# Hybrid retention and RG-LRU decoder step: state growths placed inside the last gate projection, last state products ahead of the second state half, low halves of the recurrent stage on VectorE

## The chip, the cores and the metric

The kernel runs on one core of a Trainium2 chip. The metric is the device time of one launch in microseconds (us). TensorE runs the matrix products, VectorE and ScalarE the elementwise work, GpSimd a few elementwise pieces and the transfers of the states, and SyncE the transfers of the weights. In the rows, PE is TensorE, PEld its weight loads, DVE VectorE, ACT ScalarE, POOL GpSimd and SP SyncE.

## The reference, cut to what matters

One inference step of a two-layer trunk over 528 prompt tokens (16 meta tokens and 512) and 8 running sequences of 8 tokens. Each layer does the following.

```python
xn = rmsnorm(x, ln_g)
q, k, v, z_a, x_b, z_b, g_a, g_b = split(xn @ w_in)
# retention, 4 heads, dk 256, dv 512
scores = (q @ k.T) * decay
o = scores @ v + (q * gq) @ S          # S: the state of each sequence
S_new = gamma**L * S + (k * kdecay).T @ v
o_a = group_norm(o, gn_g) * silu(z_a)
# RG-LRU, width 1536, gates block-diagonal in blocks of 96
xc = conv4(x_b);  r, i = sigmoid(xc @ w_r + b_r), sigmoid(xc @ w_i + b_i)
a = exp(-8 * r * softplus(-lam));  h = scan(a, sqrt(1 - a*a) * i * xc)
x = x + (sig(g_a) * ((o_a) @ w_a) + sig(g_b) * ((h * silu(z_b)) @ w_b)) @ w_o
```

## The kernel before, in words

All 592 tokens (528 prompt, 64 sample) are held transposed, features on the partitions, in two halves of 296 columns. Every product is made in three matmuls: each fp32 operand x is split into a rounded `x_hi` and a remainder `x_lo = x - x_hi`, and the product is hi·hi + lo·hi + hi·lo (helpers `three`, L1234 to L1239, and `three_of`, L1290 to L1294). ScalarE makes the high halves by a copy, VectorE (in places GpSimd) the low halves by a subtraction.

The order of the work is written out by hand, one instruction list for each engine, joined by semaphores. Weights come as units of 128x1024 in a ring of four (`w_raw`, `w_hi`, `w_lo`): SyncE loads one as soon as the unit four places before is used, ScalarE rounds it (`split_hi`, L354), VectorE subtracts (`split_lo`, L362), and TensorE waits for that. Results go to a ring of four PSUM banks in a fixed list of jobs (`phases`, L146): job n uses bank n mod 4 and waits until job n - 4 has been read out.

**Head stage** (four heads in each of two layers, some 150 us each). TensorE runs 16 units for each head: projections 0 to 10 (q, k, v, and three quarters of the gate z), 11 (the last quarter of z), then the output product w_a. The recurrent states of the eight sequences pass through four slots of the tile `S`, in pairs. Growing a pair has two halves c = 0 and c = 1 (`grow`, L1324 on TensorE, L808 on VectorE): TensorE makes k.T v of both sequences in two PSUM banks, VectorE computes S * gamma^8 + that in place, and TensorE may make the next product only when VectorE has read the one before (`grown_free`). After half c = 1 GpSimd stores the pair and loads the next two states into the same slots (L439 to L447). The product of the queries with the states (`cross`, L1311) accumulates in its own bank `o_last`, two sequences at a time: pairs 0 and 1 early, pairs 2 and 3 late. In the old order TensorE does, after projection 10: `grow(1, 0)` (L1376), `inner` 0 and 1 (the scores times v of the prompt blocks), `grow(1, 1)` (L1381), `inner` 2 and 3, the scores times v for `o_last`, `prompt_state(0)`, `cross(2)`, `prompt_state(1)`, `cross(3)` (L1408 to L1411), then four transposed blocks `oT` of the normalized output (L1413 to L1419), projection 11 in two halves with `oT` 4 between, and w_a. VectorE, beside it: the silu of z (L819), `grow` 1,0 (L954), the variance of output blocks 0 and 1, `grow` 1,1 (L984), the variance of blocks 2 and 3 (`variance`, L956), normalization of blocks 0 to 3, the variance of block 4 (the rows of `o_last`), then `gate` (L977), which multiplies `oT` with silu(z) and frees the bank. ScalarE copies both halves of the prompt state, and then `o_last` (L615 to L621).

**Recurrent stage** (two passes `it` of two groups `g` in each layer). TensorE makes three projections for the convolution and three for the gate z_b (six units), and then the block-diagonal gate products (L1453 to L1467), which wait for the low halves of the gate weights (`gwl_ready`) and of the convolved tiles (`xcl_ready`). ScalarE copies the projections out, rounds `xc_hi` and `gw_hi`, and evaluates tanh, sigmoid, exp and sqrt. VectorE makes the convolution (`conv`, L1081: a TENSOR_SCALAR at L1094, then three SCALAR_TENSOR_TENSOR) and the silu (L1108, which frees the bank of z_b) in the order conv 0, conv 1, silu 0, conv 2, silu 1, silu 2, then the products with the gates and the scans (L1125 to L1157). GpSimd makes `gw_lo` (L482, 128x1792) and three `xc_lo` (L487, 128x592 each) for each group, and loads the gate weights (`load_gates`, L470).

Then come the gates g_a and g_b, the w_b product and the output product w_o, which the change does not touch.

Of the kernel before, what the change touches and what calls it, by code (L numbers as in the profile page):

```python
# [27 lines left out]
D_MODEL, DEPTH, SEQ, N_META = 1024, 2, 512, 16  # L28
DEC_BATCH, DEC_SEQ, PAST_LEN = 8, 8, 4096
HEADS, DK, DV = 4, 256, 512  # L30
# [10 lines left out]
LT = LRU // P  # L41
GROUPS = 4
# [141 lines left out]
def trunk(nc, x_in, w_units, gate_w, packs, final_gain, consts, decay, state_ret,  # L184
          y_out, ret_p, ret_s, conv_out, h_out):
    f32, f32r = mybir.dt.float32, mybir.dt.float32r
# [5 lines left out]
    with ctx:  # L192
# [144 lines left out]
        def apart(eng):  # L337

            eng.sem_inc(passed, 1)
# [60 lines left out]
        def _(pool):  # L400
# [14 lines left out]

            for l in range(DEPTH):
                pool.wait_ge(xn_ready, l * KT + KT)
                pool.wait_ge(x_stored, l * 16 + 16)
                apart(pool)
                pool.memset(qz[:, :, :], 0.0).then_inc(qz_clear, 1)  # L420
                for h in range(HEADS):
                    hh = l * HEADS + h
# [55 lines left out]
                load_gates(1)  # L478
                for g in range(GROUPS):
                    pool.wait_ge(gwh_ready, l * GROUPS + (g + 1))  # L480
                    apart(pool)
                    pool.tensor_tensor(gw_lo[:, g % 2, :, :], gw[:, g % 2, :, :],  # L482
                                       gw_hi[:, :, :].bitcast(f32), SUB).then_inc(gwl_ready, 1)
                    for t in range(3):
                        pool.wait_ge(xch_ready, l * LT + g * 3 + (t + 1))
                        apart(pool)
                        pool.tensor_tensor(xc_lo[:, t, :], xc[:, t, :], xc_hi[:, t, :].bitcast(f32), SUB)\  # L487
                            .then_inc(xcl_ready, 1)
                    if g + 2 < GROUPS:
                        load_gates(g + 2)  # L490
                pool.wait_ge(ob_ready, l * LT + LT)
# [24 lines left out]
        def _(act):  # L516
# [17 lines left out]

            for l in range(DEPTH):
                root(l + 1)
# [4 lines left out]

                for h in range(HEADS):
                    hh = l * HEADS + h
# [71 lines left out]
                    for c in range(2):  # L615
# [3 lines left out]
                        act.drain().then_inc(sp_ready, 1)  # L619
                    act.wait_ge(o_last_full, hh + 1)  # L620
                    act.activation(o_tok[:, 4, :], o_last[:, :], ACT.Copy).then_inc(oraw_ready, 1)  # L621
                    for k, piece in enumerate(PIECES):
# [13 lines left out]
                act.activation(tiny[:, 1, :], tiny[:, 0, :], ACT.Exp, scale=-1.0).then_inc(lamexp_ready, 1)  # L636
                for it in range(2):
                    for g in range(2):
# [65 lines left out]
                for ph in ("GA", "GB"):  # L704
                    if ph == "GB":
                        act.wait_ge(ob_ready, l * LT + LT)
                        for k in range(LT):
                            act.activation(ob_hi[:, k, :], ob[:, k, :], ACT.Copy).then_inc(obh_ready, 1)
                    for it in range(2):
                        for i in range(4):  # L710
                            for n, (a, b) in enumerate(HALVES):
                                name = (("proj", i), n)
                                if ph == "GB":
                                    act.wait_ge(ga_used, l * 16 + it * 8 + (i * 2 + n + 1))
                                wait_job(act, ph, l, it, name)
                                apart(act)
                                act.activation(sg[:, ds(it * 4 + i, 1), a:b].rearrange("p o t -> p (o t)"),
                                               psum_of(ph, name)[:, 0:HALF], ACT.Tanh, scale=0.5)\
                                   .then_inc(freed(ph, name), 1)
                                act.drain().then_inc(ga_ready if ph == "GA" else gb_ready, 1)  # L720
                            split_hi(act, ph, l, it, i)
                done = 0
                for m in range(KT):
# [5 lines left out]
                    if m % 2 == 0 or m == KT - 1:  # L729
                        split_hi(act, "B", l, 0, done)  # L730
                        done += 1
                for it in range(2):
                    for i in range(4):
                        n = l * KT + it * 4
                        act.wait_ge(sqs_ready, n + (KT + i - 1))
                        act.wait_ge(x_ready, n + (KT + i + 1))
                        apart(act)
                        act.activation(sq[:, i % 2, :], xT[:, ds(it * 4 + i, 1), :].rearrange("p o t -> p (o t)"),
                                       ACT.Square).then_inc(sq_ready, 1)
                        split_hi(act, "O", l, it, i)  # L740
# [4 lines left out]
        def _(dve):  # L745
# [30 lines left out]

            for l in range(DEPTH):
                dve.drain()
# [25 lines left out]

                for h in range(HEADS):
                    hh = l * HEADS + h
# [24 lines left out]
                    for i in range(11):  # L831
                        if i < 4:
# [31 lines left out]
                            if i == 3:  # L864
                                dve.wait_ge(ret_stored, hh + 1)
                                dve.memset(ks_src[:, :, 24:32].bitcast(f32), 0.0)
                                dve.memset(vs_src[:, :, :, 24:32].bitcast(f32), 0.0)
                                for c in range(2):
                                    dve.tensor_tensor(
                                        ks_tmp[:, c * 8:c * 8 + 8, :],  # L870
                                        qk[:, 2 + c, TP:T].rearrange("p (b x) -> p b x", b=8),
                                        cst[:, ds(h * DEC_SEQ + C_GK, DEC_SEQ)].rearrange("p (o x) -> p o x", o=1)
                                        .to_broadcast([P, 8, 8]), MUL)
                                dve.drain().then_inc(kg_ready, 1)
                        elif i >= 8:
                            silu(i)
# [76 lines left out]
                        if i == 10:  # L953
                            grow(1, 0)  # L954

# [25 lines left out]

                    for j in range(2):
                        variance(j, False)
                    grow(1, 1)  # L984
                    variance(2, False)
                    variance(3, True)
# [90 lines left out]

                for it in range(2):
                    for g in range(2):
# [28 lines left out]
                        def silu(t):  # L1108
# [8 lines left out]
                            split_lo(dve, "L", l, it, g * 6 + 3 + t)  # L1117

                        conv(0)
                        conv(1)  # L1120
                        silu(0)
                        conv(2)
                        silu(1)
                        silu(2)
                        for t in range(3):  # L1125
# [32 lines left out]

                for it in range(2):
                    for i in range(4):  # L1160
# [7 lines left out]
                for k in range(LT):  # L1168
                    dve.wait_ge(obh_ready, l * LT + (k + 1))
                    dve.tensor_tensor(ob_lo[:, k, :], ob[:, k, :], ob_hi[:, k, :].bitcast(f32), SUB)\  # L1170
                       .then_inc(obl_ready, 1)
                for it in range(2):
                    for i in range(4):
                        split_lo(dve, "GB", l, it, i)
# [28 lines left out]
                apart(dve)  # L1203
                for it in range(2):
                    part = sqs[:, ds(it, 1), :].rearrange("p o t -> p (o t)")
# [27 lines left out]
        def _(pe):  # L1233
# [62 lines left out]
            pe.wait_ge(const_in, 32)  # L1296
            for l in range(DEPTH):
                square_sums(l)
                for h in range(HEADS):
                    hh = l * HEADS + h  # L1300
# [34 lines left out]
                    project_first("R", l, h, xn_ready)  # L1335
                    for i in range(2, 11):
                        project("R", l, h, ("proj", i), i)
# [24 lines left out]
                        if i == 9:  # L1362
# [3 lines left out]
                            for n, (j, a, b) in enumerate(SCORE_JOBS):  # L1366
# [7 lines left out]
                                done("R", name, ins)  # L1374
                            grow(0, 1)
                    grow(1, 0)  # L1376
                    pe.wait_ge(vtok_ready, hh + 1)
                    pe.wait_ge(sc_ready, hh + 1)
                    for i in range(4):
                        if i == 2:  # L1380
                            grow(1, 1)  # L1381
                        name = ("inner", i)
# [25 lines left out]
                    prompt_state(0)  # L1408
                    cross(2)
                    prompt_state(1)  # L1410
                    cross(3)  # L1411
                    pe.wait_ge(on_ready, hh * 2 + 1)
# [34 lines left out]

                for it in range(2):
                    for g in range(2):
# [18 lines left out]
                for ph in ("GA", "GB"):  # L1468
                    for it in range(2):
                        for i in range(4):  # L1470
                            project(ph, l, it, ("proj", i), i)
                waited = 0
                for m in range(KT):
# [3 lines left out]
                    for n, (a, b) in enumerate(HALVES):  # L1477
# [8 lines left out]
                        done("B", name, ins)  # L1486
                for it in range(2):
                    project_first("O", l, it, mgl_ready)
                    for i in range(2, 4):
                        project("O", l, it, ("proj", i), i)  # L1490
# [106 lines left out]
```

## Time and profile before

| What | before |
|---|---|
| median of three runs | 2171.89 us (2171.14 to 2172.06) |
| the profiled execution | 2171.74 us |
| its span | 2169.9 us, 34433 instructions |
| TensorE busy | 2079.1 us (96%), mean granted clock 0.988 |
| VectorE, ScalarE, GpSimd busy | 1203.2, 757.4, 250.1 us |

How to read it: the span runs from the first to the last instruction of the profiled execution, which took 1.8 us more than its span. A row of a timeline gives the start, the duration, the engine, the line, the operation and its tiles, and in brackets how long the engine sat idle before it and for whom. Matmuls overlap, so a matmul's duration is longer than the distance to the next one's start.

### The profile page before, as it was taken

How to read it: one execution, taken by the hardware profiler on the slowest of the kernel's cores; microseconds unless marked ns; L12 is line 12 of the kernel's file. 1: busy time of each engine (PE TensorE's matmuls, PEld its weight loads, DVE VectorE, ACT ScalarE, POOL GpSimd, SP SyncE). 2: the span in 40 equal slices, each digit the busy share in tenths (PEclk: the TensorE clock that was granted, in tenths of full speed). 3: DMA queues.
4: the chain of work that ended last, by engine and by line, in shares of the span. 5: the costliest groups of instructions: out<-in, count | busy, mean ns of one | idle time of the engine just before them, and what ended most of it. 6: DMA issues, size and time to landing. Idle time of an engine off the chain costs nothing.

```text
span 2169.9 us, 34433 instructions
## 1 busy us (share of the span) xinstructions
PE 2079.1 (96%) x14368; PEld 1945.7 (90%) x14368; DVE 1203.2 (55%) x2035; ACT 757.4 (35%) x1260; POOL 250.1 (12%) x247
## 2 busy tenths in 40 slices
PE   4999999999999999999989999999999999999997
PEld 4979979889799999999988898997997998999996
DVE  5455455454557777524474555545646677763345
ACT  3421322322325655422233223233232355654222
POOL 1021020020112211000000201202102211100000
PEclk8999999999999999999999999999999999999998
DMA  5234243233342211322232333333423421232223
GB/s 214 69 122 156 71 135 139 101 113 122 117 156 76 76 59 59 132 69 88 88 142 95 115 131 122 109 111 108 170 64 126 151 76 66 69 113 78 69 98 139
DMA packets 60267, 234.04 MB, mean 108 GB/s; under 512 B 6944, under 2 KB 6944, under 8 KB 59472
## 3 DMA queue, kind: packets, MB, share of 16 engines
q1 hardware_dynamic: 37584, 137.41, 18.9%
q0 software_dynamic: 22528, 94.43, 12.0%
q8 instruction: 113, 1.85, 0.3%
q14 instruction: 42, 0.34, 0.1%
HBM read 183.92 MB, written 47.89 MB: 107 GB/s over the span
## 4 chain that ended last, share of the span: by engine, by line
PE 83%; DVE 6%; ACT 4%; DVEq 3%; issue 2%; ACTq 1%; DMA 1%; SPq 0%
PE bank L1237 23%; PE bank L1239 22%; PE bank L1238 22%; PE bank L1292 4%; PE bank L1294 3%; PE bank L1293 3%; PE o_last L1319 3%; DVEq L1145 2%; DVE rr L1149 2%; PE sums L1331 1%; PE bank L1308 1%; ACT rr L698 1%; DMA w_raw<-in_w_units 1%; ACTq L697 1%; DVE ct L1098 1%
## 5 line engine op out<-in xcount | busy, mean ns | idle before, releaser
L1237 PE MATMUL bank<-xn_hi,w_hi 128*128 128x296 f32 x3072 | 927.3, 302 | 47.8 <-DVE xn_lo L788 22.1
L1239 PE MATMUL bank<-xn_lo,w_hi 128*128 128x296 f32 x3072 | 922.9, 300 | 0.0
L1238 PE MATMUL bank<-xn_hi,w_lo 128*128 128x296 f32 x3072 | 919.9, 299 | 0.0
L1237 PEld LDWEIGHTS bank<-xn_hi,w_hi 128*128 128x128 f32 x3072 | 582.5, 190 | 71.3 <-issue 57.4
L1238 PEld LDWEIGHTS bank<-xn_hi,w_lo 128*128 128x128 f32 x3072 | 583.3, 190 | 0.0
L1239 PEld LDWEIGHTS bank<-xn_lo,w_hi 128*128 128x128 f32 x3072 | 580.9, 189 | 0.0
L366 DVE TENSOR_TENSOR w_lo<-w_raw,w_hi 128x1024 fp32r<-128x1024 f32 x248 | 311.4, 1256 | 336.6 <-ACT w_hi L360 332.9
L360 ACT ACTIVATE w_hi<-w_raw 128x1024 fp32r<-128x1024 f32 x248 | 261.6, 1055 | 323.5 <-DMA w_raw<-in_w_units 317.5
L1237 PE MATMUL bank<-oa_hi,w_hi 128*128 128x296 f32 x512 | 156.7, 306 | 0.0
L1239 PE MATMUL bank<-oa_lo,w_hi 128*128 128x296 f32 x512 | 153.6, 300 | 0.0
L1238 PE MATMUL bank<-oa_hi,w_lo 128*128 128x296 f32 x512 | 152.4, 298 | 0.0
L435 POOL DMA_DIRECT2D out_ret_s<-S x64 | 45.7, 717 | 849.2 <-DVEq L817 848.8
L1239 PE MATMUL bank<-ob_lo,w_hi 128*128 128x296 f32 x384 | 115.2, 300 | 0.0
L1237 PE MATMUL bank<-ob_hi,w_hi 128*128 128x296 f32 x384 | 114.6, 298 | 0.0
L1238 PE MATMUL bank<-ob_hi,w_lo 128*128 128x296 f32 x384 | 114.2, 297 | 0.0
L1237 PEld LDWEIGHTS bank<-oa_hi,w_hi 128*128 128x128 f32 x512 | 96.3, 188 | 7.8 <-issue 7.7
L1037 DVE TENSOR_TENSOR acc<-bank,acc 128x296 f32<-128x296 f32 x128 | 58.9, 465 | 71.0 <-PE bank L1239 70.2
L1238 PEld LDWEIGHTS bank<-oa_hi,w_lo 128*128 128x128 f32 x512 | 96.7, 189 | 0.0
L1239 PEld LDWEIGHTS bank<-oa_lo,w_hi 128*128 128x128 f32 x512 | 96.5, 188 | 0.0
L814 DVE SCALAR_TENSOR_TENSOR S<-S,cst,sums 128x512 f32<-128x512 f32 x128 | 89.8, 743 | 1.7 <-PE sums L1331 1.7
L565 ACT ACTIVATE vo<-bank 128x296 f32<-128x296 f32 x64 | 26.7, 417 | 152.8 <-PE bank L1239 152.0
L826 DVE SCALAR_TENSOR_TENSOR zz<-zz,bank 128x296 f32<-128x296 f32 x64 | 29.6, 462 | 79.2 <-ACT zz L550 78.3
(204 smaller groups left out, 2753.0 us busy)
## 6 DMA issues: line engine op xcount, KB each, us to landing
w_raw<-in_w_units SPq DMA_DIRECT2D x251, 512.0 KB, 3.3
S<-in_state_ret POOLq DMA_DIRECT2D x64, 512.0 KB, 4.7
out_ret_s<-S POOLq DMA_DIRECT2D x64, 512.0 KB, 4.0
gw<-in_gate_w POOLq DMA_DIRECT2D x8, 896.0 KB, 5.3
x_scr<-xT POOLq DMA_DIRECT2D x3, 2368.0 KB, 8.3
xT<-x_scr POOLq DMA_DIRECT2D x2, 2368.0 KB, 11.3
out_ret_p<-Sp POOLq DMA_DIRECT2D x8, 512.0 KB, 3.9
dec<-in_decay POOLq DMA_DIRECT2D x9, 264.0 KB, 3.2
```

The source lines that it names most:

```text
L360: act.activation(w_hi[:, n % RING, :], w_raw[:, n % RING, :], ACT.Copy).then_inc(unit_hi, 1)
L366: dve.tensor_tensor(w_lo[:, n % RING, :], w_raw[:, n % RING, :], w_hi[:, n % RING, :].bitcast(f32), SUB).then_inc(unit_lo, 1)
L435: pool.dma_start(dst, S[:, s, :, :]).then_inc(s_out[s], 16)
L814: dve.scalar_tensor_tensor(S[:, s, c, :], S[:, s, c, :], cst[:, ds(h + C_G8, 1)], grown[i][:, :], MUL, ADD).then_inc(grown_free, 1)
L1037: dve.tensor_tensor(acc[:, m, a:b], psum_of("R", name)[:, 0:HALF], acc[:, m, a:b], ADD)\
L1237: pe.matmul(ps, w_hi[:, slot, cols], x_hi, start=first, stop=False)
L1238: pe.matmul(ps, w_lo[:, slot, cols], x_hi, start=False, stop=False)
L1239: return pe.matmul(ps, w_hi[:, slot, cols], x_lo, start=False, stop=last)
L1292: pe.matmul(ps, left_hi, right_hi, start=first, stop=False)
L1293: pe.matmul(ps, left_lo, right_hi, start=False, stop=False)
L1294: return pe.matmul(ps, left_hi, right_lo, start=False, stop=last)
L1319: ins = pe.matmul(o_last[at:at + QUAD, :], qz[:, c, b * QUAD:b * QUAD + QUAD], S[:, s, c, :], start=(n < 4 and c == 0), stop=(n >= 4 and c ...
```

## The change

In the head stage, projection 10 is made half by half on TensorE, with `grow(1, 0)` between the halves and `grow(1, 1)` after the second; VectorE takes its parts of the two growths right after the silu of the first half and after the weight subtraction that follows the second. `cross(3)` comes directly after `cross(2)`, ahead of `prompt_state(1)`, and ScalarE copies `o_last` between the two halves of the prompt state. In the recurrent stage the four subtractions of a group (`gw_lo` and three `xc_lo`) leave GpSimd's list and stand in VectorE's, between the convolutions and the silus; GpSimd keeps only the loads of the gate weights. In a number of loops `range(n)` is written `range(0, n)`, which counts the same; these lines are left out here.

```diff
@@ GpSimd
                 load_gates(0)
                 load_gates(1)
-                for g in range(GROUPS):
-                    pool.wait_ge(gwh_ready, l * GROUPS + (g + 1))
-                    apart(pool)
-                    pool.tensor_tensor(gw_lo[:, g % 2, :, :], gw[:, g % 2, :, :],
-                                       gw_hi[:, :, :].bitcast(f32), SUB).then_inc(gwl_ready, 1)
-                    for t in range(3):
-                        pool.wait_ge(xch_ready, l * LT + g * 3 + (t + 1))
-                        apart(pool)
-                        pool.tensor_tensor(xc_lo[:, t, :], xc[:, t, :], xc_hi[:, t, :].bitcast(f32), SUB)\
-                            .then_inc(xcl_ready, 1)
-                    if g + 2 < GROUPS:
-                        load_gates(g + 2)
+                load_gates(2)
+                load_gates(3)
@@ ScalarE
                         act.drain().then_inc(sp_ready, 1)
-                    act.wait_ge(o_last_full, hh + 1)
-                    act.activation(o_tok[:, 4, :], o_last[:, :], ACT.Copy).then_inc(oraw_ready, 1)
+                        if c == 0:
+                            act.wait_ge(o_last_full, hh + 1)
+                            act.activation(o_tok[:, 4, :], o_last[:, :], ACT.Copy).then_inc(oraw_ready, 1)
@@ VectorE
+                        elif i == 10:
+                            silu(i, (0,))
+                            grow(1, 0)
+                            silu(i, (1,))
                         elif i >= 8:
                             silu(i)
...
                         if i == 10:
-                            grow(1, 0)
+                            grow(1, 1)
...
-                    for j in range(2):
+                    for j in range(3):
                         variance(j, False)
-                    grow(1, 1)
-                    variance(2, False)
                     variance(3, True)
...
+                        def low_xc(t):
+                            dve.wait_ge(xch_ready, gg * 3 + (t + 1))
+                            dve.tensor_tensor(xc_lo[:, t, :], xc[:, t, :], xc_hi[:, t, :].bitcast(f32), SUB)\
+                               .then_inc(xcl_ready, 1)
+
                         conv(0)
                         conv(1)
                         silu(0)
+                        low_xc(0)
                         conv(2)
+                        low_xc(1)
                         silu(1)
+                        dve.wait_ge(gwh_ready, gg + 1)
+                        dve.tensor_tensor(gw_lo[:, g, :, :], gw[:, g, :, :], gw_hi[:, :, :].bitcast(f32), SUB)\
+                           .then_inc(gwl_ready, 1)
+                        low_xc(2)
                         silu(2)
@@ TensorE
-                    for i in range(2, 11):
+                    for i in range(2, 10):
                         project("R", l, h, ("proj", i), i)
...
+                    project("R", l, h, ("proj", 10), 10, (0,))
                     grow(1, 0)
+                    project("R", l, h, ("proj", 10), 10, (1,))
+                    grow(1, 1)
...
                     for i in range(4):
-                        if i == 2:
-                            grow(1, 1)
                         name = ("inner", i)
...
                     prompt_state(0)
                     cross(2)
+                    cross(3)
                     prompt_state(1)
-                    cross(3)
```

## Rows read from the trace of the kernel before

**Rows 1.** The profile's page: busy time of each engine, share of the span, instructions.

```profile
PE 2079.1 (96%) x14368; PEld 1945.7 (90%) x14368; DVE 1203.2 (55%) x2035; ACT 757.4 (35%) x1260; POOL 250.1 (12%) x247
```

**Rows 2.** TensorE's waits: line, waited for; us in total, times, longest us.

```profile
PE bank L1237 <- DVE w_lo L366: 12.3, 4, 5.0
PE sums L1331 <- DVE S L814: 10.5, 8, 1.3
PE bank L1237 <- DVE zl L1114: 7.1, 4, 1.8
PE bank L1237 <- DVE oa L979: 6.1, 8, 0.8
```

**Rows 3.** TensorE's timeline, first head: both old growths, then `prompt_state(1)`.

```profile
122.65 0.50 PE L1331 MATMUL sums<-vst,kst 24*128 24x512 f32 x2
...
125.03 0.40 PE L1294 MATMUL bank<-vtok_lo,sc_hi 128*128 128x512 f32 x1
126.75 0.50 PE L1331 MATMUL sums<-vst,kst 24*128 24x512 f32 x2 [1.32 <-DVE S L814]
...
141.16 0.50 PE L1292 MATMUL bank<-vtok_hi,ktok_hi 128*128 128x512 f32 x1
```

**Rows 4.** VectorE's timeline, first head.

```profile
121.06 0.46 DVE L826 SCALAR_TENSOR_TENSOR zz<-zz,bank 128x296 f32<-128x296 f32 x1
...
125.29 1.40 DVE L814 SCALAR_TENSOR_TENSOR S<-S,cst,sums 128x512 f32<-128x512 f32 x2
...
128.83 1.41 DVE L814 SCALAR_TENSOR_TENSOR S<-S,cst,sums 128x512 f32<-128x512 f32 x2
...
147.60 0.69 DVE L959 BATCH_NORM_STATS2 stats<-vo 128x6 f32<-128x512 f32 x1 [7.18 <-ACT vo L621]
```

**Rows 5.** GpSimd's timeline, first head: the second pair of states.

```profile
130.90 1.43 POOL L435 DMA_DIRECT2D out_ret_s<-S  x2 [6.65 <-DVEq L817]
...
136.58 0.72 POOL L430 DMA_DIRECT2D S<-in_state_ret  x1 [0.46 <-issue]
```

**Rows 6.** Landing times of transfers: L430 in 134 to 139 us; all of `S`.

```profile
DMA to landing us min/median/max: 3.7/4.3/4.9
...
DMA to landing us min/median/max: 3.2/4.3/10.5
```

**Rows 7.** TensorE's timeline, recurrent stage of the first layer.

```profile
720.27 0.37 PE L1237 MATMUL bank<-xn_hi,w_hi 128*128 128x296 f32 x1 [1.76 <-DVE zl L1114]
...
763.44 0.61 PE L1237 MATMUL bank<-xn_hi,w_hi 128*128 128x296 f32 x1 [4.99 <-DVE w_lo L366]
```

**Rows 8.** Windows: length; busy (instructions) of PE, PEld, DVE, ACT, POOL; granted clock, DMA.

```profile
763.40:785.50 22.10, 22.06 (x145) 22.06 (x146) 18.28 (x24) 7.33 (x11) 5.87 (x3) 0.88 0.16 49
870.99:890.30 19.31, 19.31 (x142) 19.31 (x143) 8.44 (x14) 4.79 (x8) 1.57 (x3) 1.00 0.60 232
```

**Rows 9.** GpSimd's timeline, second group of the first layer.

```profile
701.69 4.16 POOL L482 TENSOR_TENSOR gw_lo<-gw,gw_hi 128x1792 fp32r<-128x1792 f32 x1 [13.88 <-ACT gw_hi L667]
...
720.75 2.21 POOL L487 TENSOR_TENSOR xc_lo<-xc,xc_hi 128x592 fp32r<-128x592 f32 x1 [4.24 <-ACT xc_hi L673]
```

**Rows 10.** VectorE's timeline, the same stretch.

```profile
701.86 4.62 DVE L1140 TENSOR_TENSOR ii<-ii,rr 128x592 f32<-128x592 f32 x1
...
710.51 0.60 DVE L1094 TENSOR_SCALAR ct<-xpad,lp 128x616 f32<-128x616 f32 x1
...
713.95 1.22 DVE L366 TENSOR_TENSOR w_lo<-w_raw,w_hi 128x1024 fp32r<-128x1024 f32 x1
...
719.66 0.83 DVE L1114 SCALAR_TENSOR_TENSOR zl<-zl,bank 128x296 f32<-128x296 f32 x2
...
721.73 1.57 DVE L1094 TENSOR_SCALAR ct<-xpad,lp 128x616 f32<-128x616 f32 x1
```

**Rows 11.** VectorE's lines by form: busy, mean ns | idle before.

```profile
L947 DVE TENSOR_TENSOR sc_lo<-sc,sc_hi 128x1600 fp32r<-128x1600 f32 x8 | 14.6, 1825 | 2.1 <-ACTq L608 2.1
L1170 DVE TENSOR_TENSOR ob_lo<-ob,ob_hi 128x592 fp32r<-128x592 f32 x24 | 16.6, 772 | 0.2
```

More of the change, by code:

```diff
@@ L414, in power @@
                                    ALU.pow).then_inc(rsd_ready, 1)
-            for l in range(DEPTH):
+            for l in range(0, DEPTH):
                 pool.wait_ge(xn_ready, l * KT + KT)
@@ L420, in _ @@
                 pool.memset(qz[:, :, :], 0.0).then_inc(qz_clear, 1)
-                for h in range(HEADS):
+                for h in range(0, HEADS):
                     hh = l * HEADS + h
@@ L533, in _ @@
                 act.activation(w_hi[:, i, :], w_raw[:, i, :], ACT.Copy).then_inc(unit_hi, 1)
-            for l in range(DEPTH):
+            for l in range(0, DEPTH):
                 root(l + 1)
@@ L540, in _ @@
                 act.wait_ge(x_stored, l * 16 + 16)
-                for h in range(HEADS):
+                for h in range(0, HEADS):
                     hh = l * HEADS + h
@@ L636, in _ @@
                 act.activation(tiny[:, 1, :], tiny[:, 0, :], ACT.Exp, scale=-1.0).then_inc(lamexp_ready, 1)
-                for it in range(2):
+                for it in range(0, 2):
                     for g in range(2):
@@ L708, in _ @@
                             act.activation(ob_hi[:, k, :], ob[:, k, :], ACT.Copy).then_inc(obh_ready, 1)
-                    for it in range(2):
+                    for it in range(0, 2):
                         for i in range(4):
@@ L731, in _ @@
                         done += 1
-                for it in range(2):
+                for it in range(0, 2):
                     for i in range(4):
@@ L775, in _ @@
                 dve.tensor_tensor(w_lo[:, i, :], w_raw[:, i, :], w_hi[:, i, :].bitcast(f32), SUB).then_inc(unit_lo, 1)
-            for l in range(DEPTH):
+            for l in range(0, DEPTH):
                 dve.drain()
@@ L802, in _ @@
                 apart(dve)
-                for h in range(HEADS):
+                for h in range(0, HEADS):
                     hh = l * HEADS + h
@@ L1076, in _ @@
                 dve.tensor_scalar(lam_nc[:, :], u[5], -LRU_C, None, MUL).then_inc(par_ready, 1)
-                for it in range(2):
+                for it in range(0, 2):
                     for g in range(2):
@@ L1157, in _ @@
                                .then_inc(ob_ready, 1)
-                for it in range(2):
+                for it in range(0, 2):
                     for i in range(4):
@@ L1171, in _ @@
                        .then_inc(obl_ready, 1)
-                for it in range(2):
+                for it in range(0, 2):
                     for i in range(4):
@@ L1203, in _ @@
                 apart(dve)
-                for it in range(2):
+                for it in range(0, 2):
                     part = sqs[:, ds(it, 1), :].rearrange("p o t -> p (o t)")
@@ L1296, in _ @@
             pe.wait_ge(const_in, 32)
-            for l in range(DEPTH):
+            for l in range(0, DEPTH):
                 square_sums(l)
-                for h in range(HEADS):
+                for h in range(0, HEADS):
                     hh = l * HEADS + h
@@ L1446, in _ @@
                 apart(pe)
-                for it in range(2):
+                for it in range(0, 2):
                     for g in range(2):
@@ L1468, in _ @@
                 for ph in ("GA", "GB"):
-                    for it in range(2):
+                    for it in range(0, 2):
                         for i in range(4):
@@ L1486, in _ @@
                         done("B", name, ins)
-                for it in range(2):
+                for it in range(0, 2):
                     project_first("O", l, it, mgl_ready)
```

## The prediction

> **What bounds the kernel now.** I read the page first: TensorE is busy 96% of the span and VectorE 55% [rows 1], so a change that leaves the matmuls as they are can only win what TensorE waits. The next view is therefore who TensorE waits for [rows 2]. Four kinds of wait lie in the stages that the change touches, 36.0 us in all: for the growth on VectorE (8 times, once in each head), for `gate` (8), for the silu of the recurrent stage (4) and for low halves of weights (4, of which two are 5.0 us long). Then the timelines around each wait. In a head, TensorE stands before the second growth until VectorE has read the first [rows 3], and VectorE reads it late because that stands behind both silus and a weight subtraction of projection 10 [rows 4]. Further on, VectorE sits idle 7.18 us for ScalarE's copy of `o_last` [rows 4], which comes after `cross(3)`; the variance of block 4 then stands in front of `gate`, and projection 11 waits for the bank that `gate` frees, 6.1 / 8 = 0.76 us [rows 2]. In the recurrent stage TensorE waits 1.76 us for a silu and 4.99 us for a weight [rows 7]. VectorE is the late one there, and two of its rows say why: a 128x592 product took 4.62 us [rows 10] where another subtraction of that size takes 0.77 [rows 11]. It was issued 0.17 us after GpSimd began its `gw_lo` of 4.16 us [rows 9] and ended 0.6 us after that one's end. L1094 took 0.60 us once, and 1.57 where it met an `xc_lo` that ran from 720.75 to 722.96 us; it ended 0.3 us after that [rows 9, 10]. So GpSimd's subtractions hold VectorE up, by 4.62 - 0.77 = 3.85 us and by 0.97 us.
>
> **How a wait becomes lost time.** The idle time is counted from the modelled end of the matmul before. A 296-column matmul starts 19.31 / 142 = 0.136 us after the one before [rows 8] and lasts about 0.30, so a wait there costs its idle time and 0.16 more: 1.92 us for the silu and 5.15 us for the weight [rows 7]. The other two weight waits are (12.3 - 10.0) / 2 = 1.15 us idle [rows 2], 1.31 us lost. Among 512-column matmuls the step is 0.136 x 512 / 296 = 0.235 us, and across the wait for the growth 126.75 - 125.03 = 1.72 us pass [rows 3]: 1.49 us lost.
>
> **Part 1, the growths inside projection 10.** Nothing is added; the same four matmuls and four VectorE operations of a head move. TensorE's first growth came after projection 10 at 122.65 us and took 0.43 us to the next start (0.50 [rows 3] less the overlap); now it lies between the halves, so TensorE stands before the second growth at 122.65 + 0.43 = 123.1 us. VectorE was free for the silu of the first half at 121.06 us [rows 4]; the growth follows it some 0.4 us later and takes 1.40 us [rows 4]: read at 122.9. The 1.49 us goes, by a margin of 0.2 us, so tenths may come back. Behind the growths on VectorE stands the variance, and that has cover: VectorE idles there later anyway [rows 4].
>
> **Part 2, the last state products first.** `cross(3)` comes the 15 matmuls of `prompt_state(1)` earlier, 15 x 0.235 = 3.5 us. ScalarE then copies `o_last` under them, VectorE takes the variance of block 4 in the 7.18 us that it idled [rows 4], and `gate` follows the first transposed block at once. The 0.76 us before projection 11 goes. Two things could be late next. ScalarE now waits for `o_last` ahead of its copy of the second state half, which frees the bank of `oT` 3; what covers it is `prompt_state(1)` for the wait, and for the copy only the twelve transposes of `oT` 0 to 2, which no row here prices (third rival). And `cross(3)` needs states 6 and 7. VectorE's second growth takes the place of the first, 125.29 + 0.43 us, and ends at 127.1 where it ended at 130.24 [rows 4]. GpSimd's store of the pair began at 130.90 us and its second load at 136.58 [rows 5], 5.7 us later; that load landed in at most 4.9 us more [rows 6]. All 3.1 us earlier, the states are there at 138.4 us at the latest. TensorE reaches `cross(3)` where `prompt_state(1)` began, 141.16 - 1.49 = 139.7 us [rows 3]: 1.3 us of slack, and no cost in the sum. GpSimd's `pow` for the normalization, queued behind those transfers, is 3.1 us earlier with them.
>
> Parts 1 and 2 together give 1.49 + 0.76 = 2.25 us for a head, 18.0 us for eight.
>
> **Part 3, four subtractions on VectorE.** Removed: every hold-up by GpSimd in this stage. Added to VectorE for each group: three `xc_lo` at 0.77 us [rows 11] (0.69 from start to start) and one `gw_lo` of 1792 columns. The trace has no VectorE subtraction that wide; 592 columns take 0.772 and 1600 take 1.825 us [rows 11], 1.045 ns a column, so 1.825 + 192 x 0.001045 = 2.03 us. Below it the bound is 1.83, above it the 4.16 us that GpSimd needs [rows 9]; I take 2.03, as the row of 1600 is the nearest. The wait for `gw_hi` that VectorE's list gains costs nothing: GpSimd had it at 701.69 us [rows 9], VectorE comes to it after 723. GpSimd's loads of gate weights wait for the same signal as before.
>
> What this does to TensorE, group 2 of a layer: the silu that it waited for began at 719.66 us [rows 10]. Without 3.85 and 0.97 us of hold-up (a convolution before it met an `xc_lo` too) it begins at 714.84, before TensorE wants the bank at 720.27 - 1.92 = 718.35: the wait of 1.92 us goes, twice in a layer (groups 2 and 4). Then VectorE runs silu and weight 2.07 us (721.73 - 719.66), `xc_lo` 0.69, the convolution 3.44 (713.95 - 710.51), `xc_lo` 0.69, silu and weight 2.07 [rows 10], `gw_lo` 2.03, together 10.99 us. That ends at 725.8 us; TensorE would begin the gate products at 718.35 + 48 x 0.136 = 724.9 us, so a new wait of some 0.9 us stands before them. I take 0.8, since 2.07 includes a pause ahead of a convolution that the second silu does not have. Group 1 has the slack of a stage just begun, as the four silu waits [rows 2] are those of groups 2 and 4; groups 2 to 4 pay 2.4 us. At the border of the passes the weight subtraction stands behind the scans; they start 3.85 us earlier, so of 5.15 us 1.30 remain, just what the last group shows at the next border, where GpSimd has nothing to subtract (1.31). After the long wait the granted clock was 0.88 over 22.10 us, so part of it ran at 1.2 GHz: 145 matmuls took 22.10 in place of 145 x 0.136 = 19.72 us. After the short wait it was 1.00 [rows 8]. These 2.38 us go too. A layer gains 2 x 1.92 + 3.85 + 2.38 - 2.4 = 7.7 us, both 15.3 us.
>
> **The sum.** 18.0 + 15.3 = 33.3 us off the profiled execution's 2171.74 us gives 2138.4 us. That execution is 0.15 us under the median of the runs. A measurement of this kernel can tell about 0.2%, 4.3 us, from no change.
>
> **The rivals.**
> VectorE keeps up (0.17): `gw_lo` and the `xc_lo` cause no waits at all and the border wait closes too. Then 2 x (2.4 + 1.30) = 7.4 us more go: 2131 us. For it: VectorE's stage is some tenths from meeting TensorE. Against: the 1.31 us at a border without GpSimd's work.
>
> VectorE becomes the bound of the recurrent stage (0.12): its new operations cost 4.16 us instead of 2.03, and L1094 stays at 1.57 because its slowness is its own. Then 2.1 + 1.0 us come on top in six groups, 18.7 us: 2157 us. Against: the same line took 0.60 us when GpSimd was still, and with the hold-ups gone VectorE's list for a group is shorter, not longer (3.85 + 2 x 0.97 off, 2.03 + 3 x 0.69 on). A rule of the Trainium skill speaks for it (Perfetto Trace Analysis, section Optimizing Scalar/DVE Operations): where VectorE is saturated, handing work to GpSimd may pay; by it the four subtractions stood in the right place and the time would be this rival's. The trace agrees that VectorE is the late engine here, not that GpSimd relieves it.
>
> Only half of the head's gain comes (0.07): the growth is read some tenths late or the bank of `oT` 3 is, 1 us in each head, 2146 us.
>
> The states land late (0.04), the other side: `cross(3)` starts 5.0 us sooner (3.5 and the 1.49 of part 1), the loads only 3.1 us. It decides once a load lands more than 6.2 us after its issue (4.9 of the row and 1.3 of slack). The slowest state transfer of the run took 10.5 us [rows 6]: then TensorE waits 4.3 us in each head, 34.4 us, and if the clock falls after it as it does after 4.99 us, 8 x 2.38 = 19 us more: 2138.4 + 53.4 = 2192 us, slower than before. Against: in that stretch the loads landed in 3.7 to 4.9 us [rows 6].
>
> **How the numbers follow.** The forecast as summed gets 0.60: 2138.4 us. The range takes in it, the first and the third rival, and tenths of a microsecond of error in each wait: 2129 to 2150 us. It leaves out 0.16. All cases but the last are faster by over 0.2%: 0.95, no change 0.01, slower 0.04.
>
> **What would show it.** Right: no wait of TensorE for L814 and `gate` left; the head's repeat 2.2 us shorter; L1140 at 0.78 and L1094 at 0.60 us throughout; waits of TensorE for the gates' low halves of about 0.8 us in three groups of four; 1.3 us at each border with the clock at 1.00 after it. Wrong: a wait of the products with `S` for the transfer, a `gw_lo` on VectorE well over 2.1 us, or gate waits of several microseconds.

## The result and the profile after

The changed kernel takes 2122.1 us (median of four runs, 2121.34 to 2122.95) against 2171.73 us of the kernel before, a median of four too: ratio 0.9772, with a 95% interval of 0.9755 to 0.9789. That is 49.6 us less where 33.3 were forecast, and below the range's lower end of 2129. The profiled execution took 2121.34 us, its span is 2119.6. In the profile of the changed kernel TensorE's lines stand 4 (from L1417 on 5) higher and VectorE's between 9 lower and 4 higher than before.

The page and TensorE's waits (line, waited for; us in total, times, longest us), to be laid beside [rows 1, 2]:

```profile
PE 2056.9 (97%) x14368; PEld 1939.2 (91%) x14368; DVE 1188.8 (56%) x2067; ACT 758.2 (36%) x1260; POOL 169.8 (8%) x215
...
PE bank L1241 <- DVE w_lo L366: 4.6, 4, 1.1
PE bank L1296 <- DVE gw_lo L1125: 3.6, 6, 1.0
```

Same number of matmuls, and yet TensorE's busy time fell by 22.2 us, more than the 2 x 2.38 us that the prediction gave to the clock: waits alone cannot explain the gain. The waits for the growth, for `gate` and for the silu are gone, as forecast, and so are the 5.0 us waits for a weight. The new wait for `gw_lo` is there too.

Where the busy time went is seen in TensorE's lines by form, first of the kernel before, then of the changed one (busy us, mean ns | idle before):

```profile
L1319 PE MATMUL o_last<-S,qz 128*32 128x512 f32 x256 | 61.1, 598 | 0.0
```

```profile
L1323 PE MATMUL o_last<-S,qz 128*32 128x512 f32 x256 | 47.6, 598 | 0.0
```

The 256 rows of the products with the states (two rows for each of 128 matmuls; the expectations call the rows matmuls) are as long as before, 598 ns, and fill 13.5 us less of the engine's time. TensorE's timeline of the first head shows where, first before, then after:

```profile
139.32 1.91 PE L1319 MATMUL o_last<-S,qz 128*32 128x512 f32 x8
...
145.01 1.91 PE L1319 MATMUL o_last<-S,qz 128*32 128x512 f32 x8
```

```profile
118.60 0.50 PE L1335 MATMUL sums<-vst,kst 24*128 24x512 f32 x2
...
122.50 0.50 PE L1335 MATMUL sums<-vst,kst 24*128 24x512 f32 x2
137.17 1.94 PE L1323 MATMUL o_last<-S,qz 128*32 128x512 f32 x16
142.92 1.97 PE L1422 MATMUL bank<-cst,vo 128*128 128x128 f32 x16
144.64 0.38 PE L1241 MATMUL bank<-xn_hi,w_hi 128*128 128x296 f32 x1
```

The growths wait for nobody (compare 126.75 in [rows 3]), and projection 11 begins at 144.64 without a wait. From one head to the next it is 145.72 us (67.26 to 212.98), where the kernel before has 149.86 (68.05 to 217.91): 4.14 us less, and 2.25 were forecast. The eye should stop at `x16`: both crosses together take 1.94 us, where before each took 1.91 by itself. The second one is almost free. Their rows begin in steps of about 0.43 us. In the first step the kernel before has two rows that start together, and the changed one four:

```profile
139.32 0.62 PE L1319 MATMUL o_last<-S,qz 128*32 128x512 f32 x2
```

```profile
137.17 0.65 PE L1323 MATMUL o_last<-S,qz 128*32 128x512 f32 x4
```

In the recurrent stage of the first layer the waits that are left, and the windows after the border of the passes (columns as in [rows 8]):

```profile
708.31 0.40 PE L1296 MATMUL bank<-xc_hi,gw_hi 128*128 128x296 f32 x1 [0.64 <-DVE gw_lo L1125]
...
740.72 0.41 PE L1241 MATMUL bank<-xn_hi,w_hi 128*128 128x296 f32 x1 [1.14 <-DVE w_lo L366]
...
760.92 0.41 PE L1296 MATMUL bank<-xc_hi,gw_hi 128*128 128x296 f32 x1 [0.36 <-DVE gw_lo L1125]
...
812.38 0.40 PE L1296 MATMUL bank<-xc_hi,gw_hi 128*128 128x296 f32 x1 [0.64 <-DVE gw_lo L1125]
```

```profile
740.72:760.30 19.58, 19.58 (x144) 19.58 (x144) 18.58 (x26) 7.92 (x12) 0.00 (x0) 1.00 0.22 80
```

The long wait of [rows 7] has become 1.14 us, and the granted clock behind it is 1.00, that is 2.4 GHz throughout, where it was 0.88 [rows 8]. VectorE's lines by form say the same from its side:

```profile
L1144 DVE TENSOR_TENSOR ii<-ii,rr 128x592 f32<-128x592 f32 x24 | 18.5, 770 | 0.4
L1125 DVE TENSOR_TENSOR gw_lo<-gw,gw_hi 128x1792 fp32r<-128x1792 f32 x8 | 16.2, 2019 | 0.0
L1087 DVE TENSOR_SCALAR ct<-xpad,lp 128x616 f32<-128x616 f32 x24 | 14.4, 601 | 2.7 <-issue 0.4
```

`gw_lo` takes 2.02 us (2.03 were estimated), and the two lines that GpSimd held up are at 0.77 and 0.60 us throughout.

### The profile page after: what moved, and what is told of

Read it like the earlier page. It is cut to its first block, busy times and chain, and to the rows that moved or that the text cites. A ratio compares the mean times of both kernels' runs of the same rounds, so it can differ in the third digit from the quotient of the medians.

```text
span 2119.6 us, 34409 instructions
## 1 busy us (share of the span) xinstructions
PE 2056.9 (97%) x14368; PEld 1939.2 (91%) x14368; DVE 1188.8 (56%) x2067; ACT 758.2 (36%) x1260; POOL 169.8 (8%) x215
## 4 chain that ended last, share of the span: by engine, by line
PE 82%; DVE 9%; ACT 3%; DVEq 2%; issue 1%; ACTq 1%; DMA 1%; SPq 0%
PE bank L1241 22%; PE bank L1243 21%; PE bank L1242 21%; PE bank L1296 4%; PE bank L1298 4%; PE bank L1297 4%; PE o_last L1323 2%; DVE rr L1153 2%; DVE ct L1091 1%; DVE w_lo L366 1%; PE sums L1335 1%; PE bank L1312 1%; ACT rr L689 1%; DMA w_raw<-in_w_units 1%; ACTq L688 1%
## 5 line engine op out<-in xcount | busy, mean ns | idle before, releaser
L366 DVE TENSOR_TENSOR w_lo<-w_raw,w_hi 128x1024 fp32r<-128x1024 f32 x248 | 303.1, 1223 | 336.7 <-ACT w_hi L360 332.7
L1242 PEld LDWEIGHTS bank<-ob_hi,w_lo 128*128 128x128 f32 x384 | 72.4, 189 | 0.0
```

The source lines that it names most:

```text
L366: dve.tensor_tensor(w_lo[:, n % RING, :], w_raw[:, n % RING, :], w_hi[:, n % RING, :].bitcast(f32), SUB).then_inc(unit_lo, 1)
L1242: pe.matmul(ps, w_lo[:, slot, cols], x_hi, start=False, stop=False)
```

## The experiments

Two theories stood for the surplus. **T1**: the pair of `cross(2)` writes two quarters (32 rows each) of `o_last` and the pair of `cross(3)` the other two, so that next to each other their matmuls run side by side on TensorE. **T2**: `cross(3)` costs what it cost, and the surplus comes from its place, from another part or from how the parts meet.

**Each part alone, and parts 1 and 2 together.** Each kernel is the one before with the hunks of the diff that belong to the part.

> The kernel before with part 1 alone: both growths of the second pair inside and behind projection 10, nothing else moved. By the prediction's term it gains the 1.49 us of the wait for the growth in each of eight heads, 11.9 us: 2171.7 - 11.9 = 2159.8 us, and TensorE's wait for S (10.5 us in eight) is gone. If the surplus of the changed kernel (a head shortened by 4.15 us where 2.25 were forecast) came from this part, it gains 11.9 + 14.4 = 26.3 us: 2145 us.

Measured: 2160.33 us against 2171.39, ratio 0.9953 (0.9936 to 0.9969): 11.1 us less, and the wait for `S` is not in the list any more. Part 1 is what the prediction said; the surplus isn't here.

> The kernel before with part 2 alone: cross(3) directly behind cross(2), ScalarE's copy of o_last between the halves of the prompt state. Theory T1: the two crosses write different quarters of o_last, so their matmuls run beside each other and the second costs almost nothing; the gain of a head is then 0.76 us (the wait for gate) and about 1.8 us (a cross): 8 x 2.56 = 20.5 us, 2151 us, and the sixteen matmuls of both crosses together take about 1.9 us. Rival T2 (cross(3) costs the same wherever it stands, as the prediction had it): 8 x 0.76 = 6.1 us, 2166 us, and the sixteen take 3.7 us.

Measured: 2162.78 us, ratio 0.9962 (0.9948 to 0.9977): 8.6 us less, by the interval 5 to 11. That is not the 20.5 of T1, and the 6.1 of T2 is not excluded. The rows of the products fill 59.1 us, 2.0 less than before; with the 6.1 us for `gate`, whose wait is gone, that makes 8.1. The timeline of this kernel's first head says why, and so do the waits of TensorE's weight loads (us in total, times, longest us):

```profile
139.05 1.91 PE L1320 MATMUL o_last<-S,qz 128*32 128x512 f32 x10
141.50 1.90 PE L1320 MATMUL o_last<-S,qz 128*32 128x512 f32 x6 [0.55 <-DMA S<-in_state_ret]
```

```profile
PEld o_last L1320 <- DMA S<-in_state_ret: 5.9, 7, 1.5
```

Only two of the second cross's rows got beside the first's; then it stood for its other state. GpSimd's timeline of the same head shows the loads of that pair, first in this kernel, then in the changed one:

```profile
135.28 0.71 POOL L430 DMA_DIRECT2D S<-in_state_ret  x1 [3.21 <-DMA out_ret_s<-S]
136.49 0.72 POOL L430 DMA_DIRECT2D S<-in_state_ret  x1 [0.50 <-issue]
```

```profile
131.02 0.71 POOL L430 DMA_DIRECT2D S<-in_state_ret  x1 [2.38 <-DMA out_ret_s<-S]
132.86 0.72 POOL L430 DMA_DIRECT2D S<-in_state_ret  x1 [1.14 <-DMA out_ret_s<-S]
```

The wait ended at 141.50, 5.0 us after the later issue. This is the fourth rival of the prediction, at work where part 1 does not bring the loads forward. The next kernel brings them forward.

> The kernel before with parts 1 and 2 together, part 3 undone. Measured alone, part 1 gave 11.1 us, part 2 8.6 and part 3 17.6, together 37.3 of the 49.3 us of the whole. T1 (side by side crosses, which part 2 alone could not use since its cross(3) waited for state 7, 0.55 us idle in the first head): the two parts together give 49.3 - 17.6 = 31.7 us, 2139.7 us, with sixteen matmuls in about 1.9 us and no wait for a state. Rival T2 (the parts of the head add up, and the surplus lies between head and recurrent stage): 19.7 us, 2151.7 us.

Measured: 2141.35 us against 2171.98, ratio 0.9859 (0.9844 to 0.9873): 30.6 us less, by T1 31.7 and by T2 19.7. The products with the states fill 48.7 us of TensorE's time. Part 2 needs part 1. The expectation of no wait for a state failed: three are left, 0.8 us together.

> The kernel before with part 3 alone: gw_lo and the xc_lo on VectorE. By the prediction's term 2 x 7.7 = 15.3 us less, 2156.4 us; by the difference of the recurrent stages in the two traces (215.20 to 206.37 us in a layer) 17.7 us less, 2154 us. The granted clock stays at 1.00 behind the border of the passes. If part of that difference came from the other parts, it gains less than 15.3 us.

Measured: 2153.82 us against 2171.39, ratio 0.9920 (0.9905 to 0.9934): 17.6 us less. With the 30.6 us of the head that makes 48.2 of the 49.6, so the two stages add up.

**The same order, other quarters.** Begin and end of the sums in `o_last` move with it (the flags of its earlier products, left out here).

```diff
-                                at = b // 2 * QUAD
+                                at = (b // 2 - (2 if pair == 3 else 0)) * QUAD
```

> The changed kernel with cross(3) accumulated into the quarters of o_last that cross(2) writes, and the sums in o_last begun and ended elsewhere to suit, so that the rows of the samples are not the reference's. Order, number and sizes of all instructions stay. T1 (neighbours run beside each other because they write different quarters): the sixteen matmuls take 3.7 us instead of 1.94, 1.75 us more in each head, of which VectorE's part behind them may hide nothing: 8 x 1.75 = 14 us above the changed kernel's 2122.1, 2136 us. Rival T2 (being next to each other is enough, whatever the quarters): 2122 us.

Measured: 2133.73 us, 11.6 us above the changed kernel. The first head:

```profile
137.20 3.63 PE L1323 MATMUL o_last<-S,qz 128*32 128x512 f32 x16
144.60 1.97 PE L1422 MATMUL bank<-cst,vo 128*128 128x128 f32 x16
```

Same place, same sixteen rows, 3.63 us instead of 1.94, and what follows is 1.68 us later. The rows start two at a time again:

```profile
137.20 0.62 PE L1323 MATMUL o_last<-S,qz 128*32 128x512 f32 x2
```

T2 falls: being neighbours is not enough, it takes different quarters. Whether the array of TensorE or the bank sets this, no run here separates. Eight times 1.68 would be 13.4 us. Over all heads the rows fill 59.6 us here and 47.6 in the changed kernel, 12.0 us, near the 11.6 measured. The difference is that this kernel takes 3.63 us in every head, while the changed kernel doesn't reach 1.94 in all of them. In its last head a state lands late:

```profile
1614.18 2.95 PE L1323 MATMUL o_last<-S,qz 128*32 128x512 f32 x16
```

```profile
1610.62 0.71 POOL L430 DMA_DIRECT2D S<-in_state_ret  x1 [0.48 <-issue]
```

The loads of that head took 4.0 to 4.6 us to land, so the later one landed after the rows had begun. Four of the eight heads are above 1.94 (2.10, 1.99, 2.29 and 2.95), 1.6 us in all.

**The same neighbours, old place.**

```diff
                     prompt_state(0)
-                    cross(2)
                     prompt_state(1)
+                    cross(2)
                     cross(3)
```

> The kernel before with both halves of the prompt state first and cross(2), cross(3) behind them: the pair is adjacent but not earlier than before, and nothing else is moved. T1: cross(3) costs almost nothing beside cross(2), 8 x 1.75 = 14 us less than the kernel before, 2157 us; the wait for gate (0.76 us a head) stays. Rival T2 (the gain needs the early place, under which ScalarE and VectorE do the work of block 4): no change, 2171 us.

Measured: 2157.77 us against 2171.98, ratio 0.9935 (0.9920 to 0.9950): 14.2 us less by exchanging two calls, with the waits for `S` and `gate` left nearly as they were (10.5 and 6.4 us). The sixteen rows take 1.94 us in all eight heads. The early place is not needed either.

**The early crosses joined.**

```diff
-                        if i in (5, 6):
-                            if i == 5:
-                                pe.wait_ge(qk_ready, hh * 2 + 1)
-                            cross(i - 5)
+                        if i == 6:
+                            pe.wait_ge(qk_ready, hh * 2 + 1)
+                            cross(0)
+                            cross(1)
```

> The changed kernel with the early crosses joined too: cross(0) leaves its place behind projection 5 and comes directly ahead of cross(1) behind projection 6. T1: cross(1) costs almost nothing, 8 x 1.8 = 14.4 us less than the changed kernel's 2122.1, 2107.7 us. Rival T2: no change, 2122 us; or slower if the first growth, which reads the same states, is put off by the later cross(0).

Measured: 2106.17 us, ratio to the kernel before 0.9699 (0.9683 to 0.9716), 15.9 us under the changed kernel. TensorE's lines by form:

```profile
L1323 PE MATMUL o_last<-S,qz 128*32 128x512 f32 x256 | 33.1, 598 | 0.0
```

61.1, 47.6, 33.1 us with none, one and both couples joined: each is worth about 14 us. T1 foretold this gain too.

**The halves of part 3.** First `gw_lo` alone moves to VectorE, then the three `xc_lo` alone.

```diff
                         silu(1)
+                        dve.wait_ge(gwh_ready, gg + 1)
+                        dve.tensor_tensor(gw_lo[:, g, :, :], gw[:, g, :, :], gw_hi[:, :, :].bitcast(f32), SUB)\
+                           .then_inc(gwl_ready, 1)
                         silu(2)
```

> The kernel before with gw_lo alone on VectorE, behind the second silu; the three xc_lo stay on GpSimd. By the prediction's terms gw_lo is the costly one: its hold-up of 3.85 us goes and with it both silu waits (2 x 1.92 a layer), 3.85 of the border wait and 2.38 of clock; without the xc_lo in VectorE's list the gates wait little. A layer gains about 9 us, 2171.9 - 18 = 2154 us, about as much as the whole of part 3 (17.6). Rival: the xc_lo carry half of it or more, and this kernel gains 9 us or less, 2163 us or above.

Measured: 2171.01 us against 2172.34, ratio 0.9993 (0.9983 to 1.0002). The expectation of 18 us failed. TensorE's waits and then its timeline in this kernel:

```profile
PE bank L1291 <- DVE gw_lo L1121: 14.7, 7, 2.7
```

```profile
726.83 0.41 PE L1291 MATMUL bank<-xc_hi,gw_hi 128*128 128x296 f32 x1 [2.45 <-DVE gw_lo L1121]
```

VectorE's and GpSimd's timelines just before it:

```profile
723.51 3.27 DVE L1121 TENSOR_TENSOR gw_lo<-gw,gw_hi 128x1792 fp32r<-128x1792 f32 x1
```

```profile
722.71 2.19 POOL L483 TENSOR_TENSOR xc_lo<-xc,xc_hi 128x592 fp32r<-128x592 f32 x1 [4.27 <-ACT xc_hi L669]
```

And windows of the same kernel, behind that wait and behind the shorter one at the border:

```profile
726.83:748.88 22.05, 22.05 (x151) 22.05 (x152) 8.72 (x12) 14.97 (x22) 0.57 (x1) 0.92 0.18 66
...
760.73:780.26 19.53, 19.53 (x144) 19.53 (x144) 18.52 (x24) 7.80 (x12) 5.29 (x3) 1.00 0.23 81
```

The silu waits went and the border wait shrank to 1.14 us, as the terms said. But two convolutions of a group still meet an `xc_lo` (1.57 us in place of 0.60), and `gw_lo` now meets the third one itself: 3.27 us in place of 2.02. So the gates wait 2.20 to 2.74 us in three groups of a layer, and the granted clock falls behind each (0.92 over 22.05 us: part of it at 1.2 GHz; 151 matmuls take 22.05 us instead of 151 x 0.136 = 20.5).

> The kernel before with the three xc_lo on VectorE and gw_lo left on GpSimd. By the prediction's terms the hold-up of 3.85 us stays, and with it the 5.0 us wait at the border of the passes and the lower clock behind it; against 0.97 us of hold-up for each xc_lo the list gains 0.69. At best the silu waits shrink, up to 2 x 1.9 us a layer: 0 to 7.6 us less, 2164 to 2172 us. Rival: the xc_lo carry the gain, 2163 us or below.

Measured: 2171.40 us against 2172.34, ratio 0.9995 (0.9985 to 1.0004), at the lower end of what was expected. `gw_lo` on GpSimd still holds VectorE up: its product of `ii` and `rr` has a mean of 1.73 us, as in the kernel before, and 0.77 with `gw_lo` moved.

```profile
L1143 DVE TENSOR_TENSOR ii<-ii,rr 128x592 f32<-128x592 f32 x24 | 41.6, 1735 | 0.4
```

The list of TensorE's waits keeps the long weight waits and spreads the silu's:

```profile
PE bank L1240 <- DVE w_lo L366: 12.6, 4, 5.0
...
PE bank L1240 <- DVE zl L1109: 3.5, 4, 1.1
PE bank L1295 <- DVE zl L1109: 2.6, 4, 0.7
```

Each half gives about 1 us, which its interval does not tell from nothing; both together give 17.6. One half takes GpSimd's work off one place, and the other half meets VectorE in another.

**What is left.** `gw_lo` goes ahead of the weight subtraction inside `silu(1)`:

```diff
-                        silu(1)
+                        silu(1, False)
                         dve.wait_ge(gwh_ready, gg + 1)
...
+                        split_lo(dve, "L", l, it, g * 6 + 4)
                         low_xc(2)
```

> The changed kernel with gw_lo ahead of the weight subtraction of the second silu, 1.15 us earlier. If the three waits of the gate products for gw_lo (0.93, 0.66 and 0.93 us from start to start in a layer, against 0.14 without a wait) cost what they show, 2 x 2.1 = 4.2 us go: 2117.9 us. Rival: the weight subtraction that is put off is late next, and nothing is gained: 2122 us or above.

Measured: 2119.43 us, ratio to the kernel before 0.9756 (0.9742 to 0.9771): 2.7 us under the changed kernel, which these runs don't part from 4.2 with certainty. The wait for `gw_lo` is gone from the list. But in groups 2 and 4 of the first layer the thirteenth gate product now starts 0.37 and 0.38 us after the one before and not 0.14: its weight load waits for the silu that frees its bank, which VectorE does behind `gw_lo`. So some tenths of each wait have only moved.

The last kernel adds the joined early crosses, and the weight subtraction at the end of each pass ahead of the third scan:

```diff
+                            if (g, t) == (1, 2):
+                                if it == 0:
+                                    split_lo(dve, "L", l, 1, 0)
+                                else:
+                                    split_lo(dve, "GA", l, 0, 0)
                             dve.wait_ge(sqrt_ready, gg * 3 + (t + 1))
```

> The changed kernel with the early crosses joined, gw_lo ahead of that weight subtraction, and the first weight subtraction behind each pass taken ahead of the third scan instead of behind it. If the gains add up: 2106.2 - 4.2 - 4 x 1.3 (the border waits, 1.43 us from start to start against 0.14) = 2096.8 us, and no wait of TensorE is left but for xn_lo, the final gain and the square sums. Rival: the scans and convolutions put off by 1.2 us make a new wait, and it stays at 2102 us.

Measured: 2100.03 us, ratio to the kernel before 0.9667 (0.9653 to 0.9681): 22 us under the changed kernel and the fastest here, 3 us above the sum, of which 1.5 are that the gates gave 2.7 and not 4.2. The list shows the border wait gone and small ones new:

```profile
PE bank L1304 <- DVE gw_lo L1126: 1.3, 2, 0.6
PE bank L1304 <- DVE zl L1107: 0.9, 3, 0.3
```

With the 1.1 us at the border gone TensorE reaches the next gates earlier, and VectorE, which did not get faster, is late there: both waits for `gw_lo` stand in the group behind the border, 0.64 us in the first layer.

## Why the prediction was wrong, point by point

- **Part 1** was right: 11.9 us forecast, 11.1 measured alone, and the wait is gone.
- **Part 2 is the step that failed.** It let `cross(3)` come the 15 matmuls of `prompt_state(1)` earlier at an unchanged cost and priced only the wait behind it: 0.76 us in a head, 6.1 in eight. Its premise, that "a change that leaves the matmuls as they are can only win what TensorE waits", is what the runs refute: the same neighbours in the old place gained 14.2 us with the waits nearly unchanged. On top of part 1 it gave 30.6 - 11.1 = 19.5 us. Of the 13.4 us more, 12.4 are the cross that costs almost nothing beside its neighbour: 61.1 - 48.7 us of busy time in that kernel. The last 1.0 is within what medians can differ. The kernel with the same quarters confirms it, 1.69 us (3.63 - 1.94) in the first head and 12.0 over all. The trace had the hint: the row of a cross has the weight form `128*32`, and its eight rows begin two at a time, so the two sequences of a pair already ran beside each other. The prediction asked of the move only who waits, not which neighbour the matmuls get.
- The Trainium skill has the rule (TensorE: Matmul & The Clock Gate, section Why this matters for your kernels): products with few output rows whose outputs start in different 32-partition blocks run concurrently. The trace agrees: the sixteen rows of both crosses take 1.94 us on four blocks and 3.63 us on two.
- **The states' slack**, 1.3 us in the prediction, is used up. Side by side, `cross(3)` begins with `cross(2)` and not 1.9 us behind it, so the states are wanted sooner. Without part 1 the transfer was late by 0.55 us in the first head. In the changed kernel the list of TensorE's weight loads names a single wait of 0.2 us, but the sixteen rows are stretched in four heads, by 1.6 us in all. The fourth rival had the right place and, at 53 us, a far too high price.
- **Part 3** was right in its mechanism and a little small: 15.3 us forecast, 17.6 measured alone. By its steps in the first layer: the silu waits went, the border wait fell from 5.28 to 1.43 us from start to start (3.85, as forecast), the clock stays at 1.00, and the gate waits cost 0.79, 0.52 and 0.79 us in place of three times 0.8. What the sum did not have: the 84 matmuls of a gate group took 11.87, 11.68 and 11.87 us in groups 2 to 4 of the first layer and take 11.53, 11.52 and 11.54 with part 3 alone: 0.8 us in a layer. In group 2 of the kernel before, a part of it is a wait for ScalarE ahead of the 25th matmul, which the sum had nowhere:

```profile
730.48 0.19 PEld L1292 LDWEIGHTS bank<-xc_hi,gw_hi 128*128 128x128 f32 x1 [0.30 <-ACT rr L686]
```

  With part 3 the gates begin behind their own wait, and in groups 2 to 4 no such step is left; that ScalarE has caught up by then is argued, and no run here isolates it.
- **The rivals.** VectorE did not become the bound (`gw_lo` 2.02 us, not 4.16), and it did not quite keep up either: the waits of 0.8 and 1.3 us are those forecast. The rule weighed there, that a saturated VectorE may hand work to GpSimd, did not hold. The Trainium skill itself says in the same place (Perfetto Trace Analysis, section Optimizing Scalar/DVE Operations) that the two share a port and that moving work between them may not help; that half was the one that bore on this case.
- The range missed because no case in it had a gain that is not a wait. 33.3 + 13.4 (part 2, nearly all of it the cross) + 2.3 (part 3) - 0.8 (part 1) = 48.2 us, and 1.4 us of the 49.6 stays unassigned, within the differences of medians.

## What to carry to other kernels

When a product with a narrow output is moved, look at its new neighbours: narrow products that write different 32-row quarters should stand next to each other, and a busy time that shrinks at the same instruction count is the sign of it. Such a gain can hang on an operand's arrival, as here on the states, so bring the transfer forward in the same change and look at every repeat, not at the first alone. When two engines hold each other up, move all of the colliding work; half of it may give nothing.

## What the runs showed of the hardware that was not expected

- Sixteen rows on four quarters of one bank took 1.94 us, on two quarters 3.63 us. Rows on different quarters started together, four at 137.17 us in the one kernel and two at 137.20 in the other.
- A VectorE subtraction of 128x1792 took 2.02 us by itself and 3.27 when GpSimd's `xc_lo` was under way at its start. `xc_lo` ran to 722.71 + 2.19 = 724.90 us, 1.39 us after the start of `gw_lo`, and 3.27 - 1.39 = 1.88 is about its own time. The Trainium skill (SBUF — State Buffer, section SBUF: two separate sides) calls the pair of ports that both use an exclusive lock for a whole instruction; the trace agrees.
- The granted clock fell behind waits of 2.45 us (0.92 over 22.05 us) and 4.99 us [rows 7, 8], and stayed at 1.00 behind one of 1.14 us. In the kernel with `gw_lo` alone this took back part of what the shorter border wait had given.
